# A two-block transformer layer pair on one core: tap buffer, weight slots and the order of side steps

## The chip, the cores and the metric

The kernel runs on one core of a Trainium2 chip. A core has TensorE (PE: matmuls and transposes into PSUM), ScalarE (ACT), VectorE (DVE), GpSimd (POOL), and SyncE (SP), which issues the DMAs. Each engine takes its own instructions in order and waits on semaphores that the others raise. The metric is the time of one execution on the device, in microseconds (us), lower is better. PSUM has eight banks of 128 x 512 floats.

## The reference, cut to what matters

The reference takes one sequence of 256 tokens of width 2048 through two layers, all in float32. The first layer is Hyena with mLSTM:

```python
hn = rmsnorm(x, norm1_w)
proj = hn @ w_in
conv_out = centred_depthwise_conv(proj[..., :SHORT_CONV_CH], conv_w, conv_b)    # three taps
hv, hx1, hx2 = ...                       # 3 x 1024 channels of conv_out
z = hx1 * long_conv(hv, kf[:, 0], hb[0])
y_a = hx2 * long_conv(z, kf[:, 1], hb[1])
qk = silu(conv_out[..., 3 * HW:])        # 2 x 1024 channels, for the mLSTM
x = x + (gate_a * (y_a @ w_branch_a) + gate_b * (y_b @ w_branch_b)) @ w_out
x = x + (silu(gate) * up) @ w_down
x = rmsnorm(x, norm_f_w)
```

The second layer is gated linear attention (GLA) with a sparse attention (NSA):

```python
proj = rms_norm(x, attn_norm_g) @ w_in
g_qkv = silu(causal_short_conv(g_qkv, gla_conv_w))
log_a = log_sigmoid(gate_lr @ gate_w2 + gate_b) / 16      # the decay
gla_out = gla_mixer(...)                 # cumulated sums of log_a in chunks of 64
k_cmp = rms_norm(silu(flat_blocks @ w1) @ w2)    # compressed keys; values likewise
nsa_out = ...                            # compressed, selected and window attention
h = x + concat(gla_out, nsa_out) @ w_out
return h + (silu(m @ w_gate) * (m @ w_up)) @ w_down
```

## The kernel before

**Main work.** Every weight matrix is cut in tiles of 128 x 128. Sixteen tiles are one load of 1 MB into one of three RAW buffers (`raw`, on SyncE); half of it, eight tiles, is a unit. ScalarE rounds a unit to WH (`high`, line 1237), and the rest, RAW - WH, becomes WL: on VectorE for even units (`low`, line 1955), on GpSimd for odd ones (line 2854). WH and WL have four slots each. A group is an output of 256 tokens x 512 channels: two row tiles, each with its main bank, `mb(nt) = PB[nt % 3]`. Each product is made of three matmuls of 512 columns (lines 712, 713, 716: hi x WH, lo x WH, hi x WL). A group over K = 2048 is 64 tiles and 96 matmuls; its second row tile begins 8 tiles in. `main_free(nt)` waits until bank nt - 3 has been emptied.

**Order.** All engines walk the same count of tiles (`Walk`). Each engine's program says what else it does at tile k of a group, and a generator beside it (`beside`) advances one side step each 8.9 tiles in the first layer's projection and each 12.3 tiles at the start of the second layer's (rate 1.3/16). Within a tile, `high` stands at tile counts that are multiples of 8, `low` one tile later, both ahead of the other steps of that tile. At unit u they handle unit u + 3, and skip it if it is not split.

**Side banks.** The other five banks go round by turn (`wide_bank`): a turn may begin when the turn five before has been emptied. The filter transform of block b takes, in this order, `turned`, `kt` 0 and 1, the inverse of block b - 1 (emptied by `gated` on VectorE, line 2057), `bu` 0 and 1, and the filters of b + 1 (`fw` 0 and 1, lines 781 and 782).

**Taps.** Ten groups of the first projection go through the short convolution while the next group runs. `projected` (line 1550) evicts both row tiles into SIG, which is the memory of TM. `projected_split` (tiles 6 and 9) splits them into 16-bit planes PRP, two DMA transposes bring them to PRT, `projected_joined` (line 1565, tiles 42 and 45) writes TM again, `conv_middle` (line 1577, tiles 46 and 49) writes the middle tap to a side bank, two turns of which `banks_for_taps` takes at tile 36, and `conv_outer` on VectorE (lines 1989 to 1996, tiles 48 and 51) adds the outer taps. The next `projected` waits for the last of them.

**Sine.** The filter network's first layer is a matmul in side step 1 (line 800), its argument is reduced on VectorE (`reduced`, lines 2026 to 2037) in step 2, and ScalarE's sine (line 1269) follows in step 3, TensorE's second layer (line 806) in step 4.

**Second layer.** Group c0, one row tile lr (the gate's rank-16 input), group c1, og, v, kc, ks, and then the queries nq in four parts of 16 tiles, with 16 tiles of the compression weights behind each (`cmp`, line 1198). Those weights are not split: TensorE reads them from RAW, which comes free when it has. `levels` starts with og: the decay's matmuls (line 932), bias and absolute value (lines 2258, 2262), Exp and Ln (lines 1359, 1361), sums (lines 2266, 2271), and eight levels of the GLA scores. The keys' norms come at tiles 2 to 6 of nq on ScalarE, their scaling (`keys_scaled`, line 2784) at tile 9 on VectorE, and their transposes (`turn_keys`, line 730) at tile 24 on TensorE, in the second part.

**Last mixer group.** In the groups mn, x of the groups before is split, transposed by DMA, joined (`x_joined`, line 2580), normalized (line 1252) and its remainder taken (`x_remainder`, line 2599); group 2 is transposed on TensorE (`normed_turned`). `residual` (line 2616) evicts each row tile.

Of the kernel before, what the change touches and what calls it, by code (L numbers as in the profile page):

```python
# [16 lines left out]
T = 256  # L17
KB = 1024
# [106 lines left out]
def build(nc, A, out):  # L125
    with ExitStack() as ctx:
# [136 lines left out]
        PRP = at("PRP", [128, 2, 2, 512], U16, arena + 68 * KB)  # L263
        PRT = at("PRT", [128, 8, T], U16, arena + 64 * KB)
# [125 lines left out]
        def second_marks(i):  # L390

            marks = {}
            for name, j, first, of in SECOND:
                for what, k in ((("v back",), 44) if (name, j) == ("kc", 0) else (None, 0),
# [51 lines left out]
        def bank(*name):  # L446
            return sb(turns[name])

# [199 lines left out]
        def tensor(e):  # L648
# [18 lines left out]
            def ntile(o, hi, lo, ks, steps, ready=None, hooks={}):  # L667
                for n in w.tiles(len(ks)):
# [3 lines left out]
                    s, c = u % NSPL, slice(r * 128, (r + 1) * 128)  # L672
# [17 lines left out]
            def group(nt, hi, lo, K, ready=None, hooks={}, banks=None, part=None):  # L690
# [3 lines left out]
                for n in w.tiles(count):  # L694
# [10 lines left out]
                    s, x, o = u % NSPL, slice(h * 128, (h + 1) * 128), (banks[h] if banks else mb(nt + h))[:, 0:512]  # L705
# [90 lines left out]
            def hyena():  # L796
# [4 lines left out]
                         stop=True).then_inc(*hy.pe.mark(("f", 0)))  # L801
                yield from idle(3)
# [124 lines left out]
            def levels():  # L927
# [7 lines left out]
                yield  # L935
                yield from idle(2)
# [235 lines left out]
            group(NT["c1"], HNH, HNL, 16)  # L1172
# [3 lines left out]
            for name, j, first, of in SECOND:  # L1176
# [3 lines left out]
                elif name == "v":  # L1180
                    group(NT["v"] + 2 * j, HNH, HNL, 16, None,
                          {8: lambda: turn_group("vg", 0), 32: lambda: v_turned(0)} if j else {})
                elif name == "kc":
                    group(NT["kc"], HNH, HNL, 16, None, {8: lambda: turn_group("vg", 1), 32: lambda: v_turned(1)})
# [17 lines left out]
                elif name == "nq":  # L1202
                    group(NT[f"nq{j}"], HNH, HNL, 16, None, {} if j else {24: turn_keys}, None, (first, of))
# [20 lines left out]
        def scalar(e):  # L1224
            w = Walk()

            def high(u):
# [9 lines left out]
                e.activation(WH[:, u % NSPL, :], RAW[:, n % NRAW, half * SU * 128:(half + 1) * SU * 128],  # L1237
                             ACT.Copy).then_inc(*wt.act.mark(("wh", u)))
# [27 lines left out]
            def hyena():  # L1266
                yield from idle(2)
                e.wait_ge(*hy.dve.done("r", 0))
                e.activation(H2[0:64, :], HA[0:64, 2, :], ACT.Sin).then_inc(*hy.act.mark(("sin", 0)))
                filter_high(0)  # L1270
# [85 lines left out]
            def levels():  # L1356
# [3 lines left out]
                e.wait_ge(*gl.act.prev())  # L1360
                e.activation(ge, ge, ACT.Ln, bias=1.0).then_inc(*gl.act.mark("ln"))
                yield from idle(3)
# [178 lines left out]
            def projected(g):  # L1541

                for h in range(2):
# [4 lines left out]
                    else:  # L1548
                        e.wait_ge(*m.dve.done("conv", 4 * g - 1))
# [11 lines left out]
            def projected_joined(g, q):  # L1561
# [3 lines left out]
                e.activation(flat(TM[:, 2 * q:2 * q + 2, :]).bitcast(U16).rearrange("p (n s) -> p s n", s=2),  # L1565
# [3 lines left out]
            def conv_middle(g, q):  # L1569

                e.wait_ge(*m.act.done("pr joined", g, q))
                for s in (m.act, m.dve, hy.act, hy.dve):
                    if s.has("bank", turns[("pr", g, q)] - 5):
# [1581 lines left out]
```

## Time and profile before

| | |
|---|---|
| median of 3 runs | 2642.84 us (2641.39 to 2643.51) |
| profiled execution | 2642.1 us, its span 2640.3 us |
| TensorE matmul | 2611.5 us busy, 99% |
| ScalarE | 1400.9 us, 53% |
| GpSimd | 1194.1 us, 45% |
| VectorE | 1090.1 us, 41% |
| mean granted clock of TensorE | 0.997 |
| HBM read | 487.11 MB |

Busy time of TensorE includes the modelled ends of matmuls that overlap the next: matmuls of 512 columns start each 0.227 us, though a row gives 0.39 us for one. What the table shows is an average over all stages.

### The profile page before, as it was taken

Reading aid. Unit: us, or ns where it says so; the run is one execution under the profiler, and the core shown is the slowest. Engines: PE = TensorE matmul, PEld = TensorE weight load, DVE = VectorE, ACT = ScalarE, POOL = GpSimd, SP = SyncE. Lnnn points to the kernel's source line nnn. Section 1 sums busy time; section 2 is a strip of 40 time slices with the busy share of each in tenths; the row PEclk is TensorE's granted clock in tenths of the full one; section 3 lists DMA queues with packets and bytes.
Section 4 is the critical chain, followed back from the end, with each engine's and each line's share of the span. In section 5 each row is a group of like instructions: output and inputs, shape, how many; then the busy total and the mean of one; then the engine's idle time right before and its main releaser. Section 6 shows DMA issues by size and latency. Waiting matters only on the chain. (4 is left out here: it accounts for less than half of the span.)

```text
span 2640.3 us, 30245 instructions
## 1 busy us (share of the span) xinstructions
PE 2611.5 (99%) x11932; PEld 2154.8 (82%) x11932; DVE 1090.1 (41%) x1302; ACT 1400.9 (53%) x1713; POOL 1194.1 (45%) x528
## 2 busy tenths in 40 slices
PE   8999999999999999999999999999999999999999
PEld 7878888788888888888888878878888888888887
DVE  5676754534342232323333566356432222222222
ACT  7666645445465555555544565555555555555333
POOL 2667653344444444444444455333344444444443
PEclk9999999999999999999999999999999999999999
DMA  8655554466666656566666544453556666666554
GB/s 294 205 186 184 169 182 169 143 224 208 206 206 204 211 200 207 200 207 203 208 211 215 200 151 158 146 208 128 176 188 209 206 202 207 200 209 204 204 202 144
DMA packets 166141, 513.73 MB, mean 195 GB/s; under 512 B 99579, under 2 KB 102620, under 8 KB 108656
## 3 DMA queue, kind: packets, MB, share of 16 engines
q1 hardware_dynamic: 165568, 511.27, 57.8%
q8 instruction: 95, 1.56, 0.2%
q10 hardware_dynamic: 432, 0.52, 0.1%
q14 instruction: 46, 0.38, 0.0%
HBM read 487.11 MB, written 2.10 MB: 185 GB/s over the span
## 5 line engine op out<-in xcount | busy, mean ns | idle before, releaser
L2854 POOL TENSOR_TENSOR WL<-RAW,WH 128x1024 fp32r<-128x1024 f32 x441 | 1077.5, 2444 | 1427.8 <-ACT WH L1237 1427.6
L1237 ACT ACTIVATE WH<-RAW 128x1024 fp32r<-128x1024 f32 x889 | 939.0, 1058 | 1109.0 <-PE PB L716 1091.7
L1955 DVE TENSOR_TENSOR WL<-RAW,WH 128x1024 fp32r<-128x1024 f32 x448 | 609.9, 1362 | 1449.5 <-ACT WH L1237 1449.3
L712 PE MATMUL PB<-WH,HNH 128*128 128x512 f32 x2464 | 971.5, 394 | 6.6 <-ACT WH L1237 2.4
L716 PE MATMUL PB<-WL,HNH 128*128 128x512 f32 x2464 | 962.8, 391 | 8.2 <-DVE WL L1955 4.2
L713 PE MATMUL PB<-WH,HNL 128*128 128x512 f32 x2464 | 960.9, 390 | 0.0
L716 PEld LDWEIGHTS PB<-WL,HNH 128*128 128x128 f32 x2464 | 463.7, 188 | 109.2 <-POOL WL L2854 6.4
L712 PEld LDWEIGHTS PB<-WH,HNH 128*128 128x128 f32 x2464 | 463.7, 188 | 107.5 <-issue 9.1
L713 PEld LDWEIGHTS PB<-WH,HNL 128*128 128x128 f32 x2464 | 463.8, 188 | 94.3
L716 PE MATMUL PB<-WL,HDH 128*128 128x512 f32 x704 | 274.0, 389 | 0.0
L713 PE MATMUL PB<-WH,HDL 128*128 128x512 f32 x704 | 274.0, 389 | 0.0
L712 PE MATMUL PB<-WH,HDH 128*128 128x512 f32 x704 | 274.0, 389 | 0.0
L712 PEld LDWEIGHTS PB<-WH,HDH 128*128 128x128 f32 x704 | 132.2, 188 | 27.6
L716 PEld LDWEIGHTS PB<-WL,HDH 128*128 128x128 f32 x704 | 132.2, 188 | 27.4
L713 PEld LDWEIGHTS PB<-WH,HDL 128*128 128x128 f32 x704 | 132.2, 188 | 27.2
L1663 ACT ACTIVATE ZF<-ZTP 128x1024 uint16<-128x1024 uint16 x44 | 60.1, 1366 | 0.0
L1656 ACT ACTIVATE ZP<-TM 128x1024 uint16<-128x1024 uint16 x44 | 44.1, 1049 | 29.1 <-DVE TM L2682 29.1
L712 PE MATMUL PB<-WH,MXH 128*128 128x512 f32 x128 | 49.9, 390 | 0.0
L713 PE MATMUL PB<-WH,MXL 128*128 128x512 f32 x128 | 49.9, 390 | 0.0
L716 PE MATMUL PB<-WL,MXH 128*128 128x512 f32 x128 | 49.8, 389 | 0.0
L2682 DVE SCALAR_TENSOR_TENSOR TM<-PB,RTOK,TM 128x512 f32<-128x512 f32 x44 | 30.9, 744 | 0.0
L716 PEld LDWEIGHTS PB<-WL,MXH 128*128 128x128 f32 x128 | 24.0, 188 | 5.1
(368 smaller groups left out, 1900.4 us busy)
## 6 DMA issues: line engine op xcount, KB each, us to landing
RAW<-in_w_gu SPq DMA_DIRECT2D x176, 1024.0 KB, 4.7
RAW<-in_w_dn SPq DMA_DIRECT2D x88, 1024.0 KB, 4.7
RAW<-in_w_in_a SPq DMA_DIRECT2D x53, 1024.0 KB, 4.8
RAW<-in_w_in SPq DMA_DIRECT2D x45, 1024.0 KB, 4.7
RAW<-in_w_out SPq DMA_DIRECT2D x32, 1024.0 KB, 4.7
RAW<-in_w_ga SPq DMA_DIRECT2D x24, 1024.0 KB, 4.7
RAW<-in_w_gb SPq DMA_DIRECT2D x24, 1024.0 KB, 4.7
WIN<-in_win SPq DMA_DIRECT2D x8, 512.0 KB, 5.7
```

What stands on the lines that cost most here:

```text
L712: e.matmul(o, hi[:, k, x], WH[:, s, c], start=k == 0, stop=False)
L713: e.matmul(o, lo[:, k, x], WH[:, s, c], start=False, stop=False)
L716: t = e.matmul(o, hi[:, k, x], WL[:, s, c], start=False, stop=k == K - 1)
L1237: e.activation(WH[:, u % NSPL, :], RAW[:, n % NRAW, half * SU * 128:(half + 1) * SU * 128], ACT.Copy).then_inc(*wt.act.mark(("wh", u)))
L1656: e.activation(planes[:, h, :, :], halves16(src[:, h, :]), ACT.Copy).then_inc(*m.act.mark(("planes", *name, h)))
L1663: e.activation(halves16(flat(dst)), two_tiles(src, q), ACT.Copy).then_inc(*m.act.mark(("joined", *name, q)))
L1955: e.tensor_tensor(WL[:, u % NSPL, :], RAW[:, n % NRAW, half * SU * 128:(half + 1) * SU * 128], f32(WH[:, u % NSPL, :]), ALU.subtract).then ...
L2682: e.scalar_tensor_tensor(out=SIG[:, h, :], in0=mb(nt)[:, 0:512], scalar=RTOK[:, h:h + 1], in1=SIG[:, h, :], op0=ALU.mult, op1=ALU.mult).th ...
L2854: e.tensor_tensor(WL[:, u % NSPL, :], RAW[:, n % NRAW, half * SU * 128:(half + 1) * SU * 128], f32(WH[:, u % NSPL, :]), ALU.subtract).then ...
```

## The change

Five edits:

- The taps get a buffer of their own, TAP, in the memory of PRP. The middle tap goes to a main bank: group g's taps, made during group g + 1, sit in `mb(2 * g + 4)`, the bank with which group g + 2 begins, and TensorE waits there for the last of them ("taps free"). One bank holds both halves in turn. `projected` waits for no tap; `projected_split` does. Joining moves to tiles 37 and 44, the middle taps to 41 and 49, the outer to 43 and 51. The side banks' turns for taps are gone.
- The slot of a weight unit is counted over split units, and `high` and `low` handle the third split unit ahead.
- The decay's matmuls come at tile 16 of group c1, its bias at tile 26, Exp and Ln at 33 and 36, the sums at 42 and 50. The levels keep their side steps.
- The filter network's first matmul moves to tile 0 of group 1, its reduction to side step 1, its sine to side step 2.
- v transposes 32 to 36, key transposes 24 to 28, keys taken 28 and 36 to 32 and 40, v taken 36 and 38 to 40 and 42. In the last mixer group the second quarter of x is joined at 18 and 22 and normalized at 22, the third one normalized at 26, with its remainder in the next stage.

```diff
+        TAP = at("TAP", [128, 4, T], F32, arena + 68 * KB)
...
+        split = [u for u in range(units) if is_split(u)]
+        nth = {u: i for i, u in enumerate(split)}
+
+        def slot(u):
+            return nth[u] % NSPL
+
         def same_slot_before(u):
-            u -= NSPL
-            while u >= 0 and not is_split(u):
-                u -= NSPL
-            return u
+            return split[nth[u] - NSPL] if nth[u] >= NSPL else -1
+
+        def split_ahead(u):
+
+            i = nth.get(u, len(split)) + NSPL - 1
+            return split[i] if i < len(split) else units
...
+        def taps_in(g):
+
+            return NT["a"] + 2 * g + 4
...
+                if m.dve.has("taps free", nt):
+                    e.wait_ge(*m.dve.done("taps free", nt))
...
-            def banks_for_taps(g):
-
-                for q in range(2):
-                    w.turn += 1
-                    turns[("pr", g, q)] = w.turn
...
-                if 1 <= g < 11:
-                    hooks[36] = lambda: banks_for_taps(g - 1)
                 if g == 0:
                     banks = [wide_bank("a", 0), wide_bank("a", 1)]
+                elif g == 1:
+                    hooks[0] = first_filter_layer
...
-            group(NT["c1"], HNH, HNL, 16)
+            group(NT["c1"], HNH, HNL, 16, None, {16: decay_rows})
...
-                    group(NT[f"nq{j}"], HNH, HNL, 16, None, {} if j else {24: turn_keys}, None, (first, of))
+                    group(NT[f"nq{j}"], HNH, HNL, 16, None, {} if j else {28: turn_keys}, None, (first, of))
...
                     if w.i % SU == 0 and w.i >= 64:
-                        high(w.i // SU + NSPL - 1)
+                        high(split_ahead(w.i // SU))
...
                     if g == 0:
                         e.wait_ge(*m.dve.done("rstd", 0))
-                    else:
-                        e.wait_ge(*m.dve.done("conv", 4 * g - 1))
...
                 if g and h == 0:
                     e.wait_ge(landed["projected"], 32 * g)
+                    e.wait_ge(*m.dve.done("conv", 4 * g - 1))
...
-                if k in (42, 45):
-                    projected_joined(g, (k - 42) // 3)
-                if k in (46, 49):
-                    conv_middle(g, (k - 46) // 3)
-                if g >= 6 and k in (58, 60):
-                    qk_silu(g, (k - 58) // 2)
+                if k in (37, 44):
+                    projected_joined(g, (k - 37) // 7)
+                if k in (41, 49):
+                    conv_middle(g, (k - 41) // 8)
+                if g >= 6 and k in (55, 62):
+                    qk_silu(g, (k - 55) // 7)
...
+                if k == 33:
+                    decay_exp()
+                if k == 36:
+                    decay_log()
...
-                    if g == 3 and k == 24:
+                    if g == 3 and k == 22:
+                        x_normed(3, "ffn", 1)
+                    if g == 3 and k == 26:
                         normed_turned(3, "ffn", 2)
...
-                yield
                 reduced(0)
-                yield from idle(3)
+                yield from idle(4)
                 reduced(1)
...
-                    if k in (48, 51):
-                        conv_outer(g - 1, (k - 48) // 3)
+                    if k in (43, 51):
+                        conv_outer(g - 1, (k - 43) // 8)
...
+                if k == 26:
+                    decay_rows()
+                if k in (42, 50):
+                    decay_sums((0, 1) if k == 42 else (2, 3))
```

## Rows read from the trace of the kernel before

**Rows 1.** The page, busy time, share and instructions of each engine.

```profile
PE 2611.5 (99%) x11932; PEld 2154.8 (82%) x11932; DVE 1090.1 (41%) x1302; ACT 1400.9 (53%) x1713; POOL 1194.1 (45%) x528
```

**Rows 2.** TensorE's waits, by releaser: us in total, times, longest.

```profile
PE PB L716 <- DVE WL L1955: 4.2, 2, 3.8
PE PB L716 <- POOL WL L2854: 3.8, 5, 1.4
PE PB L781 <- DVE ST L2057: 2.6, 1, 2.6
...
PE PB L712 <- ACT TM L1550: 1.9, 1, 1.9
PE PB L806 <- ACT H L1269: 1.5, 1, 1.5
PE PB L712 <- DVE X L2616: 1.2, 1, 1.2
...
PE PB L730 <- DVE TM L2784: 0.9, 1, 0.9
PE PB L1160 <- ACT VY L1819: 0.9, 2, 0.4
...
PE PB L792 <- DVE QK L1996: 0.6, 1, 0.6
```

**Rows 3.** Stretches of 8 us behind waits; PEclk is the granted clock.

```profile
142.70:150.70 8.00, 7.91 (x30) 6.54 (x31) 3.41 (x3) 5.86 (x8) 2.49 (x2) 0.79 0.37 97
197.80:205.80 8.00, 7.95 (x28) 6.41 (x29) 3.25 (x5) 3.92 (x5) 0.66 (x1) 0.79 0.30 124
...
1564.40:1572.40 8.00, 7.99 (x37) 6.96 (x38) 6.15 (x4) 3.10 (x3) 8.00 (x5) 0.81 0.65 223
48.30:56.30 8.00, 7.98 (x34) 6.40 (x35) 4.89 (x10) 6.97 (x9) 2.54 (x2) 1.00 0.59 227
```

**Rows 4.** The page, GpSimd's low parts.

```profile
L2854 POOL TENSOR_TENSOR WL<-RAW,WH 128x1024 fp32r<-128x1024 f32 x441 | 1077.5, 2444 | 1427.8 <-ACT WH L1237 1427.6
```

**Rows 5.** Timeline at the start of the fifth group.

```profile
136.41 3.12 DVE L2117 TENSOR_TENSOR M<-UP,KSP 128x1024 f32<-128x1024 f32 x1
...
137.96 0.39 PE L712 MATMUL PB<-WH,HNH 128*128 128x512 f32 x1
...
141.81 0.15 DVE L1996 COPY X<-PB 128x1 f32<-128x1 f32 x1
```

**Rows 6.** Timeline before the start of the second group.

```profile
53.13 0.53 DVE L2026 TENSOR_SCALAR HA<-PB,VEC 128x256 f32<-128x256 f32 x1
...
58.57 0.39 PE L712 MATMUL PB<-WH,HNH 128*128 128x512 f32 x1
```

**Rows 7.** One line's instructions, ns min/median/max.

```profile
L2031 DVE TENSOR_SCALAR HA<-HA x2: 297/1342/2387, 43.7 to 54.0; 64x256 f32<-64x256 f32 x1, 128x256 f32<-128x256 f32 x1
```

**Rows 8.** Timeline before the start of the tenth group.

```profile
281.80 1.21 DVE L2117 TENSOR_TENSOR M<-UP,KSP 128x1024 f32<-128x1024 f32 x1
...
285.03 2.42 POOL L2854 TENSOR_TENSOR WL<-RAW,WH 128x1024 fp32r<-128x1024 f32 x1 [4.24 <-ACT WH L1237]
...
287.44 0.39 PE L712 MATMUL PB<-WH,HNH 128*128 128x512 f32 x1
```

**Rows 9.** Timeline at the first compression weights.

```profile
1714.91 1.08 PE L1198 MATMUL PB<-RAW,CB 128*32 128x128 f32 x32
...
1716.19 3.49 DVE L2784 TENSOR_TENSOR TM<-TM,KN 128x512 f32<-128x512 f32 x2
...
1720.73 1.06 ACT L1237 ACTIVATE WH<-RAW 128x1024 fp32r<-128x1024 f32 x1 [4.59 <-DMA RAW<-in_w_in]
```

**Rows 10.** VectorE's timeline in the last mixer group.

```profile
1910.10 1.23 DVE L1955 TENSOR_TENSOR WL<-RAW,WH 128x1024 fp32r<-128x1024 f32 x1 [2.39 <-ACT WH L1237]
1911.24 3.82 DVE L2599 SCALAR_TENSOR_TENSOR HNL<-HNF,VEC,HNH 128x256 fp32r<-128x256 f32 x4
```

More of the change, by code:

```diff
@@ L393, in second_marks @@
             for name, j, first, of in SECOND:
-                for what, k in ((("v back",), 44) if (name, j) == ("kc", 0) else (None, 0),
+                for what, k in ((("v back",), 48) if (name, j) == ("kc", 0) else (None, 0),
                                 (("nq ready", 0), 20) if name == "vs" else (None, 0),
@@ L934, in levels @@
                 t.then_inc(*gl.pe.mark("z"))
-                yield
-                yield from idle(2)
+            def levels():
+                yield from idle(3)
                 bb = [wide_bank("diagonal", 0), wide_bank("diagonal", 1)]
@@ L1236, in high @@
                     e.wait_ge(*wt.pe.done("unit", same_slot_before(u)))
-                e.activation(WH[:, u % NSPL, :], RAW[:, n % NRAW, half * SU * 128:(half + 1) * SU * 128],
+                e.activation(WH[:, slot(u), :], RAW[:, n % NRAW, half * SU * 128:(half + 1) * SU * 128],
                              ACT.Copy).then_inc(*wt.act.mark(("wh", u)))
@@ L1266, in hyena @@
             def hyena():
-                yield from idle(2)
+                yield
                 e.wait_ge(*hy.dve.done("r", 0))
                 e.activation(H2[0:64, :], HA[0:64, 2, :], ACT.Sin).then_inc(*hy.act.mark(("sin", 0)))
+                yield
                 filter_high(0)
@@ L1352, in mlstm, with decay_exp @@
                 yield
-            def levels():
+            def decay_exp():
                 ge = flat(GE[0][:, :, :])
@@ L1359, in levels, with decay_log @@
                 e.activation(ge, ge, ACT.Exp, scale=-1.0).then_inc(*gl.act.mark("exp"))
-                e.wait_ge(*gl.act.prev())
+            def decay_log():
+                ge = flat(GE[0][:, :, :])
+                e.wait_ge(*gl.act.done("exp"))
                 e.activation(ge, ge, ACT.Ln, bias=1.0).then_inc(*gl.act.mark("ln"))
+            def levels():
                 yield from idle(3)
@@ L1571, in conv_middle @@
                 e.wait_ge(*m.act.done("pr joined", g, q))
-                for s in (m.act, m.dve, hy.act, hy.dve):
-                    if s.has("bank", turns[("pr", g, q)] - 5):
-                        e.wait_ge(*s.done("bank", turns[("pr", g, q)] - 5))
+                if q:
+                    e.wait_ge(*m.dve.done("conv", 4 * g + 1))
                 for i in range(2):
                     j = 4 * g + 2 * q + i
-                    e.activation(bank("pr", g, q)[:, 256 * i:256 * i + 256], TM[:, 2 * q + i, :], ACT.Identity,
+                    e.activation(mb(taps_in(g))[:, 256 * i:256 * i + 256], TAP[:, 2 * q + i, :], ACT.Identity,
                                  bias=vec("cb", j), scale=vec("cw1", j)).then_inc(*m.act.mark(("cm", j)))
@@ L1616, in scalar @@
                         short_conv(9, k)
+                if g == 0:
+                    e.wait_ge(*m.dve.done("conv", 39))
                 for h in range(2):
@@ L1753, in ffn @@
                     for k in tiles(64):
-                        if k == 4 and j == 0:
-                            x_normed(stage, gain, 2 if stage == 1 else 1)
+                        if k == 4 and j == 0 and stage == 1:
+                            x_normed(stage, gain, 2)
                         if k == 18 and j == 0:
@@ L2249, in mlstm, with decay_rows @@
                 yield
-            def levels():
+            def decay_rows():
                 d = gl.dve
@@ L2263, in levels, with decay_sums @@
                                        in1=flat(GG[:, :, :]), op0=ALU.mult, op1=ALU.max).then_inc(*d.mark("abs"))
-                yield
+            def decay_sums(hs):
+                d = gl.dve
+                if 0 not in hs:
+                    for h in hs:
+                        e.tensor_tensor_scan(GB[:, h, :], RST[:, :], GG[:, h, :], 0.0, ALU.mult, ALU.add).then_inc(
+                            *d.mark(*(["gb"] if h == 3 else [])))
+                    return
                 e.wait_ge(*gl.act.done("ln"))
@@ L2269, in levels @@
                 e.wait_ge(landed["reset"], 16)
-                for h in range(4):
-                    e.tensor_tensor_scan(GB[:, h, :], RST[:, :], GG[:, h, :], 0.0, ALU.mult, ALU.add).then_inc(
-                        *d.mark(*(["gb"] if h == 3 else [])))
-                yield
+                for h in hs:
+                    e.tensor_tensor_scan(GB[:, h, :], RST[:, :], GG[:, h, :], 0.0, ALU.mult, ALU.add).then_inc(*d.mark())
+            def levels():
+                d = gl.dve
+                yield from idle(2)
                 def diagonal():
@@ L2949, in gpsimd @@
                 if k == 44 * 16:
-                    e.wait_ge(*m.act.done("pr joined", 9, 1))
+                    e.wait_ge(*m.dve.done("conv", 39))
                     e.memset(VT[:, :, :, 256:257], 1.0).then_inc(*ml.pool.mark("vt ones"))
```

63 lines of the change are left out of this document (34 added, 29 removed).

## Prediction, before any run of the changed kernel

> **What bounds the kernel now.** I read the page first, for its busy shares: TensorE is busy for 99% of the span and no other engine for more than 53% [rows 1]. So the end is set by TensorE's queue: its work is fixed, and only its waits can change. The second view is therefore that of TensorE's waits [rows 2]. Nothing in the change removes a matmul or a transpose; it moves some, and it moves work of ScalarE, VectorE and GpSimd. The sum below is thus made of waits of TensorE only: those that go and those that come. The third view is the granted clock in 8 us behind a wait [rows 3]. It reads 0.79 behind the waits of 1.95 and of 2.59 us, 0.81 behind that of 3.78, and 1.00 behind that of 1.47. A mean of 0.79 over 8 us is a loss of 0.21 x 8 = 1.7 us at the lower of the two levels (1.2 instead of 2.4 GHz). I charge it with every wait of 1.95 us or more and with none of 1.47 or less; between the two lies nothing that I can read, and there I take none.
>
> The feeding chain is: DMA into RAW, ScalarE rounds a unit into WH (1.06 us, [rows 9]), and VectorE (even units, 1.23 us, [rows 10]) or GpSimd (odd units, 2.44 us, [rows 4]) makes WL. Each unit is 12 matmuls at 0.227 us, 2.72 us. Each queue is in order, so whatever stands in front of a unit's step delays it, and the other way round.
>
> **What goes.** (1) The first filter layer moves 9 tiles (3.1 us) ahead, and its sine one side step: the 1.47 us wait for the sine goes, and the 0.42 us for the low part of the filter weights with it, which lies behind the same chain. (2) Tap banks take no turn of the side banks any more. The filter matmuls' bank five turns back is then a transform bank that ScalarE has long emptied, and not the inverse's, which VectorE empties late: 2.59 us go, with 1.7 of clock. The 0.58 us of the inverse, for a tap bank, go too. (3) Evictions no longer wait for the taps: the 1.95 us with its 1.7 of clock. (4) Exp, log and sums of the decay leave the crowded start of the second stage: 3.78 us for VectorE and 0.92 of the 3.8 for GpSimd, with (1 - 0.81) x 8 = 1.5 of clock. (5) The two waits before the v transposes, 0.9 together, and the 0.9 before the key transposes, by steps 4 tiles (1.36 us) later. (6) 1.2 us for the residual of the last mixer group. Sum: 1.47 + 0.42 + 4.29 + 0.58 + 3.65 + 6.2 + 0.9 + 0.9 + 1.2 = 19.6 us.
>
> **What comes: the tap bank.** In group g+1 the taps of group g now sit in the main bank with which group g+2 starts, so TensorE may start that group only when VectorE's last tap copy is done. Before, the copy was needed 2.7 us later (second half of the group) less one eviction of 0.7. I laid the last copy of each group beside the next start for all ten groups. In seven it is 0.5 to 6 us early, and the changed tiles leave the order of work on VectorE as it was, or put only operations in between that read PSUM, which no row shows stretched.
>
> At the fifth group the copy ends at 141.96 and the group starts at 137.96 [rows 5]. VectorE's order there is the same in both kernels (product, low part, outer taps, product, outer taps; the second product, 3.12 us long, is in the row), and it has no idle time between them, so nothing brings the copy forward. Wait 4.06 - 0.16 = 3.9, and 1.7 of clock: 5.6 us. Bounds 3.5 and 6.
>
> Second group: the start comes at 58.57, less the 1.5 won by (1), 57.0. VectorE now does the first outer taps (1.75 us) ahead of the second argument reduction, which began at 53.13 [rows 6]. It would start near 53.0. GpSimd's product for tile 48 runs from about 53.4, since ScalarE is less behind. One step of such a reduction took 297 ns alone and 2387 ns while GpSimd's product ran [rows 7]. So it ends some 2.3 us later than alone, at 58.1, and 1.75 us of taps put the last copy at 59.85: wait 2.8, clock 1.7, 4.5 us. If the two miss each other the copy ends at 57.6: 0.6 us. The nearest row is the stretched one, and the two begin within 0.4 us: I take 4.5, bounds 0.4 and 4.8.
>
> The Trainium skill has a rule for this (SBUF — State Buffer, "SBUF: two separate sides"): VectorE and GpSimd share a port pair that is an exclusive lock, held for a whole instruction, and a VectorE operation with two SBUF inputs takes it against one of GpSimd that reads SBUF. By it a VectorE step waits for the rest of a 2.4 us product; by it the sum of what comes is the 24.3 us below. Were the port shared by bandwidth, each stretch would be about half, two waits would stay under 1.95 us, and it would be some 18 us, a net of -1.6. The stretched row (8 times its length alone, not 2) agrees with the lock.
>
> Tenth group: start 287.44. Before, the product at 281.80 and its subtraction ran while GpSimd was idle until 285.03 [rows 8]. Now taps stand ahead of them, the product starts at 283.7 and GpSimd at 284.0, so one of the two waits: subtraction at 287.3, last copy 289.75. Wait 2.3, clock 1.7, 4.0 us. Bounds 0 (they miss each other) and 4.3.
>
> **What comes: the weight slots.** Between the split units of the key projection (S) lie unsplit ones (C), whose RAW slot is freed only when TensorE has used it. With slots counted over split units, a unit is rounded three split units ahead, not three units ahead. In the second half of the first S, ScalarE now stands at the unit of the third S. Its RAW is C's: C starts at 1714.91, and ScalarE got that data at 1720.73, after a wait of 4.59 us for the DMA [rows 9]. Before, other units were rounded meanwhile. Behind ScalarE waits VectorE with the low part of that unit, and behind it, on VectorE, the scaling of the keys, which ran at 1716.19. TensorE's key transposes wait for this. Now: WH 1720.73 to 1721.7, low part to 1723.0, scaling 1.4 us alone = 1724.7, or behind the product of the next odd unit = 1726.7 (in the row the pair took 3.49 us, stretched so). The second half of the pair is the one that was stretched before, now it would be the first; I take the middle, 1725.7. TensorE reaches the transposes (4 tiles later than before) at 1720.1: wait 5.6, bounds 4.6 and 6.6, clock 1.7, together 7.3 us. There is no circle, as C stands ahead of the transposes. The same reordering puts a rounding ahead of an eviction before the first S (0.3) and ahead of that of the queries, where 1.6 us come and the waits of 0.60 and 1.35 for GpSimd change to 0.9 and nothing: 0.55. Sum 8.2.
>
> **What comes: the rest.** In the last mixer group ScalarE normalizes the second quarter ahead of a unit's rounding. VectorE's remainder from 1911.24 takes 3.82 us and the joined halves end at 1916.35 [rows 10]; then 1.7 for the normalizing, 1.06 for WH, 1.23 for WL and 0.7 for the residual give 1921.0, where TensorE needs it at 1919.2: 1.75 us, bounds 0 and 2 with 1.7 of clock. The decay's sums on VectorE end about when the low part of tile 57 is due, two units later: 0.3, bounds 0 and 2.4 (one product of GpSimd). The decay matmuls cost what they did.
>
> Sum of what comes: 5.6 + 4.5 + 4.0 + 8.2 + 1.75 + 0.3 = 24.3 us. Net +4.7. The profiled execution took 2642.1 us, 1.8 more than its span and 0.7 under the median: 2646.8, or 2647.5 against the median. A measurement tells 0.2%, 5.3 us, from no change, so this is still "no change".
>
> **Rivals.** (B) The products miss each other, so that the second and tenth group start nearly on time. For it: they begin within 0.4 us of each other, and small shifts decide. Then 3.9 + 4.0 us less: 2639.6. (C) The scaling of the keys isn't caught behind the third S. The waits in the queue speak against it: it needs ScalarE to get RAW without TensorE's C. It takes 8.2 away: 2639.3; with B, 2631. (D) The other side: the low part of tile 57 comes late behind the decay's sums. If VectorE's two scans meet GpSimd's product, it is 2.4 us late at tile 16 of the next group, more than 1.95, so with the clock 4.1 instead of 0.3: 2651.3. It decides from 0.5 us of delay on. Against it: most of the sums lie where GpSimd has one product in 5.4 us.
>
> **How the numbers follow.** Forecast 0.46, B 0.22, C alone 0.05, C with B 0.07, D 0.20. Of the forecast a third ends above 2648.1 by its bounds, so slower is 0.15 + 0.20 = 0.35. Faster by over 5.3 us needs C with B or several bounds at once: 0.14. The rest, 0.51, is within 0.2%. Likeliest 2647.5, range 2637 to 2655, from B, with part of its own bounds, to D with the fifth group's and the last mixer's upper bounds.
>
> **What would show it.** After: no wait at the sine, at the filters or at og's VectorE low part; TensorE waits at the starts of groups 2, 5 and 10 for the tap copy (2.8, 3.9, 2.3), and 4.6 to 6.6 us at the key transposes, for the scaling; ScalarE idle for a DMA in the first S. The clock row below 1.00 behind each. The prediction is wrong if the copies at groups 2 and 10 are in time, or if the keys are scaled before 1722.

## The result, and the profile after

The changed kernel takes 2647.54 us (median of 22 runs, 2644.35 to 2651.39), the kernel before 2642.86 (22 runs): 4.7 us more, a ratio of 1.0018 with a 95% interval of 1.0012 to 1.0024. The ratio is inside the 0.2% that the prediction called "no change", and since the interval leaves out 1, a small loss is shown all the same. The median is 0.04 us from the predicted figure. So close a hit is luck: below, some terms are off by 2 to 4 us. All times here and below are medians of fast executions; one slow execution of reduction_first (6811 us) and one of held_waits (3903 us) are left out.

The page of the changed kernel, busy time of each engine, answers to [rows 1]:

```profile
PE 2616.8 (99%) x11932; PEld 2159.1 (82%) x11932; DVE 1082.6 (41%) x1302; ACT 1401.9 (53%) x1713; POOL 1188.4 (45%) x528
```

The same 11932 matmuls and transposes, 5.3 us more busy, since more of them ran at the lower clock (mean granted clock 0.994, before 0.997). TensorE's waits in the changed kernel (by releaser: us in total, times, longest), against [rows 2]:

```profile
PE PB L745 <- DVE TM L2825: 6.2, 1, 6.2
PE PB L727 <- issue: 3.9, 1, 3.9
PE PB L727 <- ACT TM L1821: 3.5, 2, 3.1
PE PB L727 <- DVE V L2020: 2.9, 1, 2.9
...
PE PB L731 <- POOL WL L2895: 1.9, 3, 1.1
PE PB L727 <- ACT QK L1600: 1.7, 1, 1.7
PE PB L727 <- DVE X L2648: 1.6, 1, 1.6
```

The waits that the prediction let go are gone: filters' bank, eviction, sine, inverse, VectorE's low part in og, v transposes. In their place stand the key transposes (line 745), the starts of groups 5 (the row that names no releaser), 2 and 10, and the residual of the last mixer group. One is twice as long as was said: 3.1 us for the eviction of the queries (line 1821). The granted clock in the 8 us behind five of them, windows of the changed kernel in the form of [rows 3]:

```profile
60.98:68.98 8.00, 8.00 (x28) 6.43 (x29) 2.34 (x3) 4.12 (x7) 2.49 (x1) 0.79 0.28 69
145.50:153.50 8.00, 8.00 (x26) 6.51 (x27) 1.86 (x1) 1.94 (x2) 4.08 (x2) 0.65 0.41 124
290.38:298.38 8.00, 8.00 (x37) 6.77 (x38) 4.46 (x5) 5.92 (x8) 3.18 (x2) 1.00 0.46 141
1722.34:1730.34 8.00, 8.00 (x54) 6.34 (x55) 0.00 (x0) 0.00 (x0) 0.00 (x0) 0.64 0.13 20
1745.97:1753.97 8.00, 8.00 (x29) 6.68 (x30) 0.68 (x1) 4.38 (x20) 2.38 (x1) 0.62 0.81 303
```

0.79 is the 1.7 us of the prediction; 0.65, 0.64 and 0.62 are 2.8, 2.9 and 3.0 us; the tenth group's wait of 1.7 us cost no clock. The profiled execution took 2650.72 us, 3.2 above its median, so these rows show a little more loss than a usual execution has.

Both kernels issue the same 10656 matmuls of the split units in the same order, so the start of each can be set against the start of the same one before. Worked out from TensorE's timelines, in us more (+) or less than before; columns: its time before, the changed kernel, and two runs that come below:

```
 time before   changed   slots_undone   taps_undone
      32.95     +0.87        -0.27         +0.94      group 1 starts
      58.57     +2.41        +0.78         -1.90      group 2 starts
      85.73     +3.48        +1.86         -2.07
     137.96     +7.54        +5.91         -2.07      group 5 starts
     170.26     +6.44        +4.86         -2.12
     231.45     +1.07        -0.52         -2.25
     287.44     +2.94        +1.35         -2.26      group 10 starts
    1538.94     +5.16        +3.57         -0.19      decay's matmuls now ahead of here
    1572.74     -3.70        -5.29         -9.06      og: decay's waits gone
    1709.38     -4.33        -6.49         -9.69
    1738.92     +7.05        -7.08         +0.46      keys
    1770.09     +8.19        -7.12         -1.25      queries
        end     +8.64        -6.68         -0.80
```

The +0.87 at the start of group 1 is no late start. Group 0 ends level (its last matmul is at 32.70 us, before at 32.73), and then comes the filter network's first matmul, which stood inside group 1 before and here waits a little for its weights:

```profile
33.24 0.64 PE L809 MATMUL PB<-ZT,FW 33*64 33x256 f32 x2 [0.15 <-DMA FW<-in_filt_w]
```

By 48.9 us the changed kernel is 0.6 us ahead. In this new place the matmul ties the start of group 1 to a DMA: in reduction_first, below, where group 0 ended 2.9 us earlier, the same wait is 2.15 us.

The changed kernel falls behind at two places. One is groups 2 to 5, up to +7.5; part of it comes back where the old kernel has its own waits, and +1.1 is left at 231 us, +2.9 with group 10. The other is the 60 us around the first compression weights, where it stands at -4.3 before and +8.2 behind. What happened there, ScalarE's timeline of the changed kernel (start, us, in brackets the idle time before and its releaser):

```profile
1716.53 2.00 ACT L1249 ACTIVATE WH<-RAW 128x1024 fp32r<-128x1024 f32 x2 [7.14 <-DMA RAW<-in_w_in]
1733.24 1.06 ACT L1249 ACTIVATE WH<-RAW 128x1024 fp32r<-128x1024 f32 x1 [14.71 <-DMA RAW<-in_w_in]
```

and VectorE's:

```profile
1717.62 1.23 DVE L1979 TENSOR_TENSOR WL<-RAW,WH 128x1024 fp32r<-128x1024 f32 x1 [11.94 <-ACT WH L1249]
1718.76 0.20 DVE L2821 RECIPROCAL KN<-KN 128x8 f32<-128x8 f32 x1
1718.99 3.20 DVE L2825 TENSOR_TENSOR TM<-TM,KN 128x512 f32<-128x512 f32 x2
```

VectorE stands 11.9 us for ScalarE's rounding, which stands 7.1 us for its DMA; only then come the low part and, behind it, the scaling of the keys, until 1722.2. TensorE's transposes begin at 1722.34 after 6.24 us. ScalarE next stands 14.7 us for the RAW that TensorE has yet to read.

### The profile page after: what moved, and what is told of

It is laid out like the page before. It is cut to its first block and busy times, and to the rows that moved or that the text cites. A ratio compares the mean times of both kernels' runs of the same rounds, so it can differ in the third digit from the quotient of the medians.

```text
span 2648.9 us, 30220 instructions
## 1 busy us (share of the span) xinstructions
PE 2616.8 (99%) x11932; PEld 2159.1 (82%) x11932; DVE 1082.6 (41%) x1302; ACT 1401.9 (53%) x1713; POOL 1188.4 (45%) x528
```

## The experiments

Ratios are to the kernel before, with 95% intervals; each group of runs had its own runs of before (medians 2642.1 to 2643.2). The diffs show the lines that matter; where a run builds on another run, only what is new in it is shown.

**slots_undone.** The changed kernel with the slots counted over all units:

```diff
-            return nth[u] % NSPL
+            return u % NSPL
...
-                        high(split_ahead(w.i // SU))
+                        high(w.i // SU + NSPL - 1)
```

> The changed kernel with its weight slots counted over all units again, all else kept. Theory of the record (the slots put a rounding that stands for a DMA ahead of the keys' scaling): the keys' wait, 0.3 and 0.55 go, 8.2 us with the clock, so 2639.3. Read from the changed kernel's own trace instead, more hangs on the slots: the keys' wait 6.2 with a clock of 0.71 over the 10 us behind it (2.9), the wait of 3.1 for the queries' eviction at 1745.97 with a clock of 0.62 over 8 us (3.0), and some 1.1 in three short waits, less the 1.95 of GpSimd's waits of before, which come back: 14 us, so 2633. Rival (the keys are late for another reason, VectorE's or GpSimd's own work, and the slots are innocent): 2647, with a wait of 5 us or more still at the key transposes.

Measured 2635.17 us, ratio 0.9975 (0.9964 to 0.9986): 12.4 less than the changed kernel, and faster than the kernel before. The key transposes and the queries' eviction are in none of its waits. By the medians the slots cost more than the 8.2 of the record and less than the 14 read from one profile.

**slots_alone.** The same lines, the other way round, as the only edit of the kernel before.

> The kernel before with only the slot edit. Theory: with the key transposes at tile 24 and not 28, TensorE is 1.4 us earlier, so it waits 7 to 8 us for the keys' scaling, with 3 of clock; the eviction of the queries and its clock as in the changed kernel, 6. Sum near 15 us: 2657. By the terms of the record alone (8.2 + 1.4): 2652. Rival (innocent slots): 2643.

Measured 2654.72 us, ratio 1.0045 (1.0032 to 1.0058): 12.2 us more. TensorE waits 7.7 us at the key transposes and 1.7 for the queries' eviction. The 12.2 lie between the 9.6 of the record's terms and the 15 of the theory. Added to the old kernel or taken from the new one, the edit is worth the same 12 us, so it needs none of the others for its harm.

**keys_ahead.** The changed kernel, keys scaled one tile earlier, ahead of the low part in VectorE's queue:

```diff
-                        if k == 9:
+                        if k == 8:
                             keys_scaled()
```

> The changed kernel with the keys' scaling one tile earlier, tile 8 and not 9, which puts it ahead of the low part in VectorE's queue; nothing else differs. Theory (the queue's order is what makes the keys late, not a lack of weights): the wait of 6.2 us at the key transposes goes with its 2.9 of clock, and the wait at the queries' eviction stays: 9 less, 2638.5. Rival (TensorE is short of weights there, since ScalarE stands 14.7 us for RAW, and the keys only show it): the wait moves to the next unit of queries, and the time falls by under 3 us: 2645 or more.

Measured 2637.55 us, ratio 0.9980 (0.9971 to 0.9989): 10.0 less than the changed kernel, by one digit. VectorE's timeline of this run:

```profile
1709.21 1.29 DVE L2825 TENSOR_TENSOR TM<-TM,KN 128x512 f32<-128x512 f32 x2
1717.29 1.23 DVE L1979 TENSOR_TENSOR WL<-RAW,WH 128x1024 fp32r<-128x1024 f32 x1 [6.79 <-ACT WH L1249]
```

The scaling is done at 1710.5, in 1.29 us and not 3.20, and the low part comes 7 us later, in time for its unit. TensorE was never short of weights at the transposes: what made the keys late was the order of two steps in VectorE's queue, the first of which waits, through ScalarE, for a DMA. The wait for the queries' eviction stays (2.4 us), behind a rounding on ScalarE in the same way; it had no clock loss here.

**taps_undone.** The changed kernel with the taps as in the kernel before: joined in TM, in two turns of the side banks, at the old tiles. One line of the edit:

```diff
-                e.activation(mb(taps_in(g))[:, 256 * i:256 * i + 256], TAP[:, 2 * q + i, :], ACT.Identity,
+                e.activation(bank("pr", g, q)[:, 256 * i:256 * i + 256], TM[:, 2 * q + i, :], ACT.Identity,
```

> The changed kernel with the taps as before (joined in the memory of the eviction, side banks, old tiles), all else kept. Theory: the waits at the starts of groups 2, 5 and 10 go (2.9, 3.9 and 1.7 us in the changed kernel's trace, with 1.7 and 2.3 us of clock behind the first two: 12.5), and the eviction's 1.95 with 1.7, the filters' 2.59 with 1.7 and 0.58 for the inverse come back (8.5): 4.0 less, 2643.5; by the record's own terms 14.1 less 8.5, 5.6 less: 2642. Rival (the main bank costs nothing, the starts would be late anyway): those waits stay and the old ones are added, 2656.

Measured 2640.82 us, ratio 0.9996 (0.9987 to 1.0004): 6.7 less than the changed kernel; the record's terms give 5.6. The three waits at the starts are gone, and 1.94, 2.59 and 0.60 us are back, those of [rows 2] to within 0.02. In the table above its column runs level from 58 to 231 us, where the changed kernel climbs by 5 and gives back what those waits had cost.

**decay_alone.** The kernel before with the decay's edit only. VectorE's part of it:

```diff
+                if k == 26:
+                    decay_rows()
+                if k in (42, 50):
+                    decay_sums((0, 1) if k == 42 else (2, 3))
```

> The kernel before with the decay's edit alone. Record: 3.78 + 0.92 + 1.5 of clock go and 0.3 comes, 5.9 less: 2636.9. Read from the aligned traces of the changed kernel: 8.9 us less in the first group of the second stage and 2.2 more in the group ahead of it, of which the decay's own matmuls are a part: 6.6 less, 2636.3. Rival (the low part of tile 57 comes late behind the sums): 2641. Rival (the first group of the second stage is short of VectorE for another reason): 2642.

Measured 2635.48 us, ratio 0.9971 (0.9961 to 0.9982): 6.9 less; the record says 5.9. No wait for a low part stands in og. Rival D, a late tile 57, is refuted.

**mixed_banks.** The slots undone, and the taps of groups 0, 3 and 8 back in side banks, those of the other seven in the idle main bank:

```diff
+        SIDE = (0, 3, 8)
+
+        def taps_bank(g, q):
+            return bank("pr", g, q) if g in SIDE else mb(taps_in(g))
```

> The changed kernel with the slots counted over all units (2635.2), and the taps of groups 0, 3 and 8 in two side banks again, those of the other groups in the idle main bank; the taps' own buffer stays for all. Theory (a start of a group waits for the tap copy only because the taps sit in its bank): the waits of 2.9, 3.9 and 1.7 us at the starts of groups 2, 5 and 10 go with 4.0 of clock behind the first two, and neither the eviction's nor the filters' wait of the kernel before comes back: 12.5 less, 2622.7. Rival 1 (the three pairs of turns bring the filters' wait of 2.59 back with its clock): 2627. Rival 2 (VectorE's lateness is what counts, wherever the taps sit): the waits move on by half a group, 2632 or more.

Measured 2626.24 us, ratio 0.9940 (0.9927 to 0.9954): 16.2 us under the kernel before and 21.3 under the changed one. TensorE's largest waits in it:

```profile
PE PB L728 <- POOL WL L2904: 3.3, 4, 1.4
PE PB L793 <- DVE W3L L2076: 2.8, 1, 2.8
PE PB L724 <- DVE X L2657: 1.6, 1, 1.6
```

The time alone would also fit rival 1 (2627); the waits decide. Those at the starts of groups 5 and 10 are gone, and the old 2.59 at the filters' bank has not come back. Of the one of group 2 only the place has changed: TensorE starts the group in time and waits 2.8 us at its first filter matmuls, with a clock of 0.79 behind it: for this group rival 2 holds. So the edit brought 8.9 us where 12.5 were expected. The lateness in group 2 is what reduction_later, reduction_first, first_taps_late and filter_low_early are about.

**reduction_later.** The second argument reduction and its sine one side step later, behind all the outer taps (on slots_undone):

```diff
-                yield from idle(4)
+                yield from idle(5)
                 reduced(1)
```

> The changed kernel with the slots counted over all units (2635.2), and the second argument reduction with its sine one side step later, behind the outer taps and not between them. Theory (the start of the second group waits since the reduction, stretched by GpSimd's product, stands ahead of the last taps): the wait of 2.9 us goes with its 1.7 of clock, 4.6 less, 2630.6. Rival (the taps themselves are late, by their joining on ScalarE): the last copy moves by less than 1 us, 2634 or more. Second rival (the sine becomes the late one): a new wait at the filter matmuls, 2633 to 2637.

Measured 2633.75 us, ratio 0.9969 (0.9956 to 0.9981), 1.4 under slots_undone, within the uncertainty of both. The start of group 2 no longer waits, so it was the reduction ahead of the taps that held them; but the filter matmuls now wait 1.92 us, with a clock of 0.79. The second rival.

**reduction_first.** On mixed_banks, the first outer taps of group 0 at tile 48, behind the reduction:

```diff
-                    if k in (43, 51):
-                        conv_outer(g - 1, (k - 43) // 8)
+                    if k in ((48, 51) if g == 1 else (43, 51)):
+                        conv_outer(g - 1, int(k == 51))
```

> The kernel with mixed banks (2626.2), and the first outer taps of group 0 at tile 48 and not 43, so that VectorE does the second argument reduction ahead of them, as in the kernel before; nothing waits for those taps, since they sit in a side bank. Theory (VectorE's order at this place, not the bank, makes the sine and with it the low part of the filter weights late): the reduction starts 1.7 us earlier, misses GpSimd's product, and the wait of 2.83 us at the filter matmuls goes with its 1.7 of clock: 4.5 less, 2621.7. Rival (the filter weights' chain is late by ScalarE's roundings ahead of it): the wait stays above 2 us, 2625 to 2626.

Measured 2629.62 us, ratio 0.9951 (0.9938 to 0.9964): 3.4 above mixed_banks, with intervals that still touch, and 3.1 above it by the profiled spans. Theory and rival both missed the time: the filters' wait is 4.66 us. VectorE's and then GpSimd's timeline of this run:

```profile
51.30 0.30 DVE L2064 TENSOR_SCALAR HA<-HA 128x256 f32<-128x256 f32 x1
51.63 3.42 DVE L2067 SCALAR_TENSOR_TENSOR HA<-HA 128x256 f32<-128x256 f32 x3
```

```profile
52.30 2.46 POOL L2904 TENSOR_TENSOR WL<-RAW,WH 128x1024 fp32r<-128x1024 f32 x1 [2.90 <-ACT WH L1254]
```

Three steps that take 1.34 us alone took 3.42, since GpSimd's product began among them. A second product, at 59.40, met a later step of the same chain (line 2114, at 59.92), which took 2.45 us in place of 0.42.

**first_taps_late.** All steps of group 0's taps at the old tiles, so that ScalarE rounds the odd unit later and GpSimd starts behind the reduction:

```diff
+                joined, middle = ((42, 45), (46, 49)) if g == 0 else ((37, 44), (41, 49))
```

> The kernel with mixed banks (2626.2), and all steps of the taps of group 0 at the tiles of the kernel before: joined at 42 and 45, middle at 46 and 49, outer at 48 and 51. In the run that moved the outer taps alone, a product of GpSimd (52.30) met the three last steps of the reduction and another (59.40) the low part of the filters. Theory (ScalarE's early joining lets it round the odd unit 2 us later or earlier, and so sets which step of VectorE meets GpSimd's product): with the old tiles the product starts behind the reduction, as in the run with the taps undone (54.25, reduction done at 53.9), the filters' wait of 2.83 goes with its 1.7 of clock: 2621.7. Rival (the filters' chain is late wherever the taps are): a wait above 2 us stays, 2625 to 2629.

Measured 2625.71 us, ratio 0.9935 (0.9922 to 0.9949): the rival. The filters' wait stays, 2.69 us. The reduction ran in its 2.9 us as meant, and a later step on VectorE was caught instead. Its timeline, and GpSimd's:

```profile
58.51 0.42 DVE L2115 TENSOR_TENSOR HS<-H,HS 64x256 fp32r<-64x256 f32 x1
58.97 2.72 DVE L2077 TENSOR_TENSOR W3L<-W,W3H 128x512 fp32r<-128x512 f32 x1
```

```profile
58.64 2.50 POOL L2905 TENSOR_TENSOR WL<-RAW,WH 128x1024 fp32r<-128x1024 f32 x1 [2.38 <-ACT WH L1254]
```

**mixer_back.** As first_taps_late, with the last mixer group's edit undone:

```diff
-                    if g == 3 and k == 22:
-                        x_normed(3, "ffn", 1)
-                    if g == 3 and k == 26:
+                    if g == 3 and k == 24:
                         normed_turned(3, "ffn", 2)
```

> As the kernel first_taps_late, and the last mixer group's edit undone as well. Record: that edit costs 1.75 and saves 1.2, so 0.55 less than first_taps_late; by the aligned traces 0.44: 2621.3. Rival (normalizing the second quarter ahead saves time in the next stage, where it is no longer done): 1 us or more above first_taps_late.

Measured 2625.85 us, ratio 0.9934 (0.9922 to 0.9947): no difference that can be measured. In the profiles the wait is 1.20 us with the edit undone and 1.63 with it, 0.43 apart.

**filter_low_early.** As first_taps_late, the low part of the first filter weights ahead of the reduction:

```diff
                 reduced(0)
-                yield from idle(4)
+                yield from idle(3)
+                filter_low(0)
+                yield
                 reduced(1)
```

> The kernel first_taps_late (2625.7), and the low part of the first filter weights two side steps earlier on VectorE, ahead of the argument reduction: in the profile VectorE has 2 us free there, its own product ending at 47.4, and GpSimd's product at 47.66 would start behind it. In first_taps_late this low part began at 58.97, met GpSimd's product of 58.64 and took 2.72 us in place of 0.69, and TensorE waited 2.69 us for it. Theory (VectorE and GpSimd keep each other from the port, so only an order in which the short step has ended before the product starts pays): the wait goes with its clock of 1.1 to 1.7: 4 less, 2621.5. Rival (VectorE's queue is simply full, and what is moved out of one place comes back at the next, as in the last two runs): 2625 or more.

Measured 2625.43 us, ratio 0.9929 (0.9915 to 0.9942): the rival again. The moved step took 0.69 us at 49.19, and the one that stayed was caught; TensorE still waits 2.23 us at the filter matmuls. VectorE, then GpSimd:

```profile
59.34 1.22 DVE L1989 TENSOR_TENSOR WL<-RAW,WH 128x1024 fp32r<-128x1024 f32 x1
60.59 2.58 DVE L2117 TENSOR_TENSOR HS<-H,HS 64x256 fp32r<-64x256 f32 x1
```

```profile
60.54 2.36 POOL L2906 TENSOR_TENSOR WL<-RAW,WH 128x1024 fp32r<-128x1024 f32 x1 [2.22 <-ACT WH L1254]
```

A step of 0.42 us takes 2.58 when GpSimd began 0.05 us before it. Four versions lie between 2625.4 and 2626.2 us, which no measurement here tells apart; the best of them, whichever it is, is 0.6 to 0.7% faster than the kernel before.

**held_waits.** On slots_undone, 14 waits of seven lengths in the first feed-forward stage:

```diff
+                    e.wait_ge(*wt.pe.done("unit", w.i // SU - 1))
...
+                            e.memset(sb(b)[:, 0:n], 0.0).then_inc(*m.dve.mark(*([] if left else [("held", i)])))
```

> The changed kernel with the slots counted over all units (2635.2), and 14 waits put into TensorE's work in the first feed-forward stage, two of each of seven lengths, each for VectorE to fill 850 to 2560 columns of idle banks; the work is else the same. It measures the clock's price of a wait by itself. By the rule of the record a wait of 1.95 us or more costs 1.7 us on top and one of 1.47 or less nothing, whatever its length: with waits of about 1.1 to 2.9 us, 27 us of waits and 6 x 1.7 of clock, 2672, with the step between 1.5 and 1.95. Rival 1 (the price grows with the length from the first, as 1.7, 2.3 and 2.9 us behind waits of 2.9, 3.9 and 6.2 in the changed kernel might say): the clock falls a little behind every one of them. Rival 2 (what decides is where in the chip's own rhythm a wait falls, not its length): the two waits of one length read differently.

It is read from its profiled execution of 2669.79 us. The waits came out at 1.08, 1.40, 1.61, 1.83, 2.04, 2.51 and 2.89 us, each twice, 26.7 in all. Windows of 8 us behind the two of 1.83, the two of 2.04, the two of 2.51 and the two of 2.89:

```profile
1050.57:1058.57 8.00, 8.00 (x28) 6.41 (x29) 1.06 (x1) 1.58 (x2) 2.40 (x1) 0.79 0.84 197
1076.10:1084.10 8.00, 8.00 (x35) 6.63 (x36) 3.25 (x3) 2.12 (x2) 2.40 (x1) 1.00 0.47 147
1100.21:1108.21 8.00, 8.00 (x35) 6.63 (x36) 2.11 (x2) 2.12 (x2) 2.40 (x1) 1.00 0.84 206
1124.32:1132.32 8.00, 8.00 (x35) 6.62 (x36) 3.24 (x3) 2.12 (x2) 2.40 (x1) 1.00 0.41 139
1148.91:1156.91 8.00, 8.00 (x35) 6.64 (x36) 2.13 (x2) 2.12 (x2) 2.40 (x1) 1.00 0.81 187
1173.48:1181.48 8.00, 8.00 (x28) 6.43 (x29) 2.19 (x2) 1.60 (x2) 2.40 (x1) 0.79 0.37 133
1200.05:1208.05 8.00, 8.00 (x35) 6.65 (x36) 2.14 (x2) 2.12 (x2) 2.40 (x1) 1.00 0.79 174
1224.99:1232.99 8.00, 8.00 (x28) 6.42 (x29) 2.19 (x2) 1.60 (x2) 2.23 (x1) 0.79 0.31 123
```

The six waits of 1.08 to 1.61 us all read 1.00. Above them, two waits of one length, some 25 us apart in one execution, read 0.79 and 1.00 in three of the four pairs, and one of 1.83 us lost where four longer ones did not. So between 1.83 and 2.89 us the length doesn't decide: the record's rule is refuted there, and so is rival 1. Rival 2 agrees with the pairs, but no run shows what does decide.

## Why the prediction was right

**Gains: the mechanisms and nearly the sizes.** The waits named under "what goes" went; at the key transposes and at the mixer's residual a longer one stands in their place, as the record says under "what comes" (1.64 us at the residual, 1.75 said). The decay edit alone is 6.9 us against 5.9.

**The fifth and second group: right.** Waits 3.95 (3.9 said) and 2.86 (2.8 said), the second with 1.7 of clock as said, the fifth with 2.8. (The record's 4.06 for the fifth is 4.00 by its own rows; it changes nothing.) In the second group both ends of the wait came 1.1 us later than drawn: TensorE was ready at 58.1 and not 57.0, the last copy done at 60.9 and not 59.85. That the difference held at 2.8 is partly luck. The reduction was stretched as drawn, VectorE's step and GpSimd's product of the changed kernel:

```profile
55.01 2.19 DVE L2053 TENSOR_SCALAR HA<-HA 128x256 f32<-128x256 f32 x1
```

```profile
54.64 2.41 POOL L2895 TENSOR_TENSOR WL<-RAW,WH 128x1024 fp32r<-128x1024 f32 x1 [2.90 <-ACT WH L1249]
```

The same step took 297 ns alone [rows 7]. In three more runs short VectorE steps that met a GpSimd product grew by 2.0 to 2.2 us each, whatever their own length: 2.58 for 0.42, 2.72 for 0.69, 3.42 for three of 1.34 in all. A shared bandwidth would have stretched them by one factor; here it is 6.1, 3.9 and 2.6. The Trainium skill's rule of an exclusive lock that is held for a whole instruction (SBUF — State Buffer, "SBUF: two separate sides") agrees with these three rows, whose steps have two inputs in SBUF. The step of line 2053 and the row from which the record took its stretch have one; for such a step the rule asks for a mode that uses both ports, and no row names the mode. Rival B (products that miss each other) did not happen in the changed kernel.

**The tenth group: mechanism right, size off.** 1.73 in place of 2.3, and none of the 1.7 of clock: the term of 4.0 measured 1.7.

**Keys: mechanism right, size a little low.** The chain ran in the predicted order, and keys_ahead shows that it is the queue's order. The wait is 6.24, inside the bounds of 4.6 to 6.6: the scaling met GpSimd's product in its first half, the later of the two cases that I took the middle of. Clock 2.9, not 1.7. Together 9.1 against 7.3, and keys_ahead takes 10.0 away by the medians. The record's sign, "scaled before 1722", is best read in the time of the kernel before, from which its numbers come: here the scaling ends at 1722.2, where the changed kernel is 4.3 us ahead, which is 1726.5 in the old time (1725.7 said). Rival C is refuted by this trace, where the scaling is caught, and by slots_undone, where it isn't.

**The queries' eviction: a term that was mis-sized, by how much is open.** The step is the 0.55 in which "1.6 us come" for a rounding ahead of the eviction of the queries, and GpSimd's 0.60 and 1.35 change to 0.9 and nothing. The wait measured 3.09 us with 3.0 of clock behind it, and GpSimd's 0.3; less the 1.95 that went, 4.4 in this profile. But in keys_ahead and taps_undone, which have the same slots, the wait is 2.4 us with a clock of 1.00 and GpSimd's is 0.3, which is 0.7 and 0.8 for the term. So the wait itself was 0.8 to 1.5 us longer than said, and the larger part of the 4.4 is a clock loss that two of the three profiles don't have. Of the 12.4 us that the slots cost by the medians, 10.0 go with the keys alone (7.3 said) and 2.4 are left (0.85 said), within the uncertainty of both runs; the keys are the larger miss. ScalarE's timeline of the changed kernel shows two roundings ahead of the eviction that each stand for RAW, 4.57 us and 1.15 us:

```profile
1740.56 1.06 ACT L1249 ACTIVATE WH<-RAW 128x1024 fp32r<-128x1024 f32 x1 [4.57 <-DMA RAW<-in_w_in]
...
1744.29 1.06 ACT L1249 ACTIVATE WH<-RAW 128x1024 fp32r<-128x1024 f32 x1 [1.15 <-DMA RAW<-in_w_in]
1745.25 1.25 ACT L1821 ACTIVATE TM<-PB,RTOK 128x512 f32<-128x512 f32 x2
```

**How it came to 2647.5.** The record said 24.3 of losses and 19.6 of gains. By the profile, the losses are 2.9 + 1.7 (group 2), 3.9 + 2.8 (group 5), 1.7 (group 10), 9.1 (keys), 0.4 (before the first S), 4.4 (queries) and 1.6 (mixer): 28.5. Two that the record lacks come on top: 0.7 in group 1, where TensorE waits 1.06 us for GpSimd's low part and not 0.39, and 0.4 in the compression weights (line 1210), where it waits for ScalarE. That is 29.6. The profiled execution stands 8.6 above the other, so the gains are 21.0. The differences between the columns of the table of matmul starts say what each edit is worth in these executions, the medians what it is worth in a usual one (us, + is slower):

```
                         record    traces    medians
taps                      +5.6      +5.4       +6.7
slots                     +8.2     +13.7      +12.4
decay                     -5.9      -6.6       -6.9
filter layer              -1.9      -2.3
v and key transposes      -1.8      -1.8
mixer                     +0.55     +0.4
sum                       +4.7      +8.8       (+4.7 measured)
```

In the traces only the slots are off by more than 1 us. The two executions lie 8.6 us apart, the medians 4.7: this execution of the changed kernel is 3.2 above its median. By the medians, 4.7 - 12.4 - 6.7 + 6.9 = -7.5 falls to the last three edits, for which record and traces say 3.2 and 3.7 less. The intervals of these runs, 1.6 to 3 us each side, add up to more than that gap of 4, so it is not resolved. What is shown is that slots and taps were priced 5.3 us too low together; what made up for it is not, and the hit within 0.04 us is luck.

## What to carry to other kernels

An engine's queue is a place where waits are inherited: before looking further ahead in it, find what each step may stand for, and put nothing that the bound engine needs soon behind a step that waits for memory which only the bound engine frees. The edits of one change are to be priced and tried one by one: here -7, +7 and +12 us hid in a "no change", and dropping one and halving another gave 0.6%. And a short VectorE step that has missed a GpSimd product is not a spare one: in the three runs that changed which step a product met, a step of the same chain was caught each time.

## What the runs showed of the hardware

What a wait costs in clock isn't a function of its length. The mean granted clock of the 8 us behind it, in the profiled executions of all kernels here but reading held_waits for its held waits alone, waits of 1.3 us or more behind 20 us:

```
wait us        clock over the next 8 us
1.35 to 1.64   1.00, 24 times
1.70 to 1.73   1.00 five times, 0.79 once (decay_alone, at 35.59,
               behind two shorter waits in the 4 us ahead of it)
1.83           0.79 once, 1.00 once
1.92 to 1.95   0.79 four times, 1.00 once
2.04           1.00 twice
2.15 to 2.23   0.79 once, 1.00 once
2.36 to 2.42   1.00 twice
2.51 to 2.59   0.79 or 0.81 seven times, 1.00 once
2.69 to 2.89   0.61 or 0.79 five times, 1.00 once
3.09 to 4.66   0.62 to 0.81, eight times
6.24 to 7.69   0.64 to 0.75, three times
```

The very same wait, 1.95 us for the eviction at 143 us, reads 0.79 in [rows 3] and 1.00 in decay_alone:

```profile
143.16:151.16 8.00, 8.00 (x44) 7.03 (x45) 3.34 (x3) 7.35 (x10) 3.94 (x3) 1.00 0.37 102
```

Up to 1.64 us nothing was lost in these rows, and from 3.09 us on always. Between, 19 of 33 rows lost, 18 of them 1.5 to 1.7 us and one 3.1, so the better term for a wait of 1.7 to 2.9 us is 1.7 us times the share of the rows that lost. What decides between them stays open. The runs were made on several chips, but the pairs of held_waits differ within one execution. In the changed kernel's long loss, matmuls behind 1746.57 start every 0.43 us instead of 0.227, which is the lower level of 1.2 GHz.
